# Moving a reload, a first norm and one weight's low parts in a two-block transformer kernel

## The reference

```python
def first_block(x, norm_gain, w_in, w_out, ...):
    xn = rms_norm(x, norm_gain)
    proj = einsum('bsd,de->bse', xn, w_in)
    qa, ka, va, za, qi, ki, wi, qb, kb, vb, zb = split(proj)
    a_out = dsa_attention(qa, ka, va, qi, ki, wi, bias_a)      # top-k chosen keys
    b_out = dilated_attention(qb, kb, vb, bias_b)
    mixed = concatenate([a_out * silu(za), b_out * silu(zb)])
    return x + einsum('bse,ed->bsd', mixed, w_out)

def second_block(x, ...):
    h = rms_norm_2(x, norm_mix)
    q_flat, kv_flat, g_attn, u_pool, g_merge = split(h @ w_in)
    a = nsa_attention(...) @ w_branch_attn
    b = pool_mixer(u_pool, pool_w, pool_scale) @ w_branch_pool
    ga, gb = split(sigmoid(g_merge))
    x = x + (ga * a + gb * b) @ w_out
    h = rms_norm_2(x, norm_mlp)
    x = x + square(relu(h @ w_ff1)) @ w_ff2
    return rms_norm_2(x, norm_final)
```

## Time and profile before

| | us |
|---|---|
| median of 3 executions | 1024.54 (1023.99 to 1026.65) |
| the profiled execution | 1024.92 |
| its span, first to last instruction | 1022.9 |
| TensorE busy | 1007.9 |
| VectorE busy | 679.3 |
| ScalarE busy | 555.7 |
| GpSimd busy | 419.5 |

### The profile page before, as it was taken

One profiled execution on the slowest core, in us unless ns is written; L12 is line 12 of the kernel. 1 busy time (PEld: TensorE's weight loads), 2 busy tenths in 40 slices (PEclk: granted clock), 3 DMA queues, 4 the chain that ended last, 5 costly groups with the idle time before them and its releaser, 6 DMA issues.

```text
span 1022.9 us, 14244 instructions
## 1 busy us (share of the span) xinstructions
PE 1007.9 (99%) x5158; PEld 828.9 (81%) x5158; DVE 679.3 (66%) x1201; ACT 555.7 (54%) x1013; POOL 419.5 (41%) x403
## 2 busy tenths in 40 slices
PE   9999999999999999999999999999999999999997
PEld 7788877778777898878887778888888888888886
DVE  5578898788975356733477879354323325999997
ACT  8455444777862356544667874224433436654555
POOL 0023012666720003900254520007779865875563
PEclk9999999999999999999999999999999999999999
DMA  9533321337140384132200461239999951444552
GB/s 338 104 98 94 103 62 42 84 84 195 54 175 1 122 272 140 42 96 69 63 1 1 143 212 58 83 119 319 343 354 338 350 191 62 150 136 147 206 185 82
DMA packets 100165, 146.24 MB, mean 143 GB/s; under 512 B 6480, under 2 KB 60496, under 8 KB 100096
## 3 DMA queue, kind: packets, MB, share of 16 engines
q1 hardware_dynamic: 86800, 130.75, 39.6%
q10 hardware_dynamic: 12768, 12.88, 4.0%
q0 software_dynamic: 528, 1.70, 1.0%
HBM read 123.69 MB, written 21.63 MB: 142 GB/s over the span
## 4 chain that ended last, share of the span: by engine, by line
PE 87%; DVE 6%; ACT 3%; issue 2%; DMA 1%; POOL 0%; SPq 0%; ACTq 0%; DVEq 0%; POOLq 0%
PE bank L966 57%; PE bank L1478 5%; PE bank L1479 5%; PE bank L1480 5%; PE bank L1358 2%; PE bank L1148 2%; PE bank L1367 2%; PE bank L1119 1%; DVE x L2242 1%; PE bank L1381 1%; DVE stats L2241 1%; DVE u_lo L2144 1%; PE bank L1132 1%; DMA wring<-in_w_in 1%; PE bank L1268 1%
## 5 line engine op out<-in xcount | busy, mean ns | idle before, releaser
L2658 DVE TENSOR_TENSOR w_lo<-wring,w_hi 128x1024 fp32r<-128x1024 f32 x32 | 50.4, 1574 | 108.5 <-ACT w_hi L1997 108.5
L2144 DVE TENSOR_TENSOR u_lo<-wring,u_hi 128x1024 fp32r<-128x1024 f32 (+2 forms) x69 | 83.3, 1215 | 53.8 <-ACT u_hi L1652 53.1
L966 PE MATMUL bank<-u_hi,h_hi 128*128 128x512 f32 (+1 forms) x288 | 110.9, 385 | 0.1
L966 PE MATMUL bank<-u_hi,h_lo 128*128 128x512 f32 (+1 forms) x288 | 109.3, 379 | 0.0
L966 PE MATMUL bank<-u_lo,h_hi 128*128 128x512 f32 (+1 forms) x288 | 109.0, 379 | 0.0
L1652 ACT ACTIVATE u_hi<-wring 128x1024 fp32r<-128x1024 f32 (+1 forms) x64 | 66.2, 1034 | 71.1 <-PE bank L966 56.1
L966 PE MATMUL bank<-h_hi,w_hi 128*128 128x512 f32 (+2 forms) x272 | 103.2, 380 | 0.0
L966 PE MATMUL bank<-h_hi,w_lo 128*128 128x512 f32 (+2 forms) x272 | 103.2, 379 | 0.0
L966 PE MATMUL bank<-h_lo,w_hi 128*128 128x512 f32 (+2 forms) x272 | 103.2, 379 | 0.0
L966 PE MATMUL bank<-h_hi,u_hi 128*128 128x512 f32 x224 | 93.5, 417 | 0.4 <-ACT arena L1594 0.2
L966 PE MATMUL bank<-h_hi,u_lo 128*128 128x512 f32 x224 | 87.8, 392 | 0.0
(11 more groups left out here) (400 smaller groups left out, 2599.0 us busy)
## 6 DMA issues: line engine op xcount, KB each, us to landing
wring<-in_w_in SPq DMA_DIRECT2D x60, 512.0 KB, 3.9
wring<-in_w_ff ACTq DMA_DIRECT2D x12, 1024.0 KB, 8.6
wring<-sums_kept SPq DMA_DIRECT2D x16, 768.0 KB, 4.2
wring<-in_w_ff SPq DMA_DIRECT2D x22, 512.0 KB, 6.4
wring<-in_w_ff SPq DMA_DIRECT2D x32, 256.0 KB, 3.4
sums_kept<-wring SPq DMA_DIRECT2D x22, 256.0 KB, 5.0
wring<-in_w_out SPq DMA_DIRECT2D x2, 2048.0 KB, 13.3
wring<-in_w_ff SPq DMA_DIRECT2D x4, 1024.0 KB, 6.9
```

What stands on the lines that cost most here:

```text
L966: last = mm(b, lhs, rhs, start=(start and n == 0), stop=(stop and n == 2))
L2144: done = v.tensor_tensor(u_lo[raw_place(u)][:, cols], raw_unit(u)[:, cols], u_hi[hi_place(u)][:, cols].bitcast(F32), ALU.subtract)
L2658: v.tensor_tensor(cut(w_lo[ring3(m)]), src, cut(w_hi[ring3(m)]).bitcast(F32), ALU.subtract).then_inc(w_lo_done, 1)
```

## The change

Three things move, and no arithmetic is changed.

1. LOW1: the two halves of the low parts of unit F0 + 7 (gate tile za 3) are made in VectorE's iterations 52 and 54; before, in 50 and 52.
2. The first block's end. ScalarE loads the square root's table before the last half of mixed_high, and squares the first tile of x after one kv2 unit; before, after three. VectorE waits for x and adds the first tile's sums before any kv2 low part; the low part of U2 follows before the first norm, those of U2 + 1 and U2 + 2 after it.
3. The reload of x for the second block. Before, SyncE issued x's four loads, and then branch units 3 to 7. Now it issues unit 3, x's tile 0, unit 4, tile 1, unit 5, tile 2, unit 6, tile 3, unit 7.

```diff
     LOW1 = {4: (F0 + 1, 0), 6: (F0 + 1, 1), 12: (F0 + 2, 0), 14: (F0 + 2, 1), 22: (F0 + 3, 0), 24: (F0 + 3, 1), 30: (F0 + 4, 0), 32: (F0 + 4, 1),
-            38: (F0 + 5, None), 44: (F0 + 6, None), 50: (F0 + 7, 0), 52: (F0 + 7, 1)}
+            38: (F0 + 5, None), 44: (F0 + 6, None), 52: (F0 + 7, 0), 54: (F0 + 7, 1)}
...
                 if name == "w2o1":
-                    sp.wait_ge(pv_done, VALUES + NS)
                     sp.wait_ge(x_out, 16 * NT)
-                    for i in range(NT):
-                        sp.dma_start(x[:, i, :], x_kept[i]).then_inc(x_back, 16)
                     for e in range(3, KC):
                         load_branch(e)
+                        if e < 3 + NT:
+                            sp.wait_ge(pv_done, VALUES + NS)
+                            sp.dma_start(x[:, e - 3, :], x_kept[e - 3]).then_inc(x_back, 16)
...
+            nc.scalar.preload_act_table(ACT.Sqrt)
             mixed_high(7, slice(S // 2, S))
-            for u in range(HI_UNITS - 1):
+            high(U2)
+            squares(NT, 0, 0)
+            for u in range(1, HI_UNITS - 1):
                 high(U2 + u)
-            for i in range(NT):
-                if i >= 1:
-                    input_high("h2", i - 1)
+            for i in range(1, NT):
+                input_high("h2", i - 1)
                 squares(NT, 0, i)
...
             mixed_low(7, slice(S // 2, S))
-            for u in range(2):
-                low(U2 + u)
             dve.wait_ge(x_in, 16 * NT)
             for i in range(NT):
                 add_x(0, i, [0])
                 if i >= 1:
                     take_halves("h2", i - 1, V_G2, h_lo)
                 add_x(0, i, [1])
+                if i == 0:
+                    low(U2)
                 norm(NT, i, xn2)
                 if i == 0:
+                    low(U2 + 1)
                     low(U2 + 2)
```

## The result

The changed kernel takes 1028.01 us (median of 7 executions, 1027.22 to 1030.78) against 1024.54 us (1023.99 to 1026.65, 7 executions): a ratio of 1.0035, with a 95% interval of 1.0023 to 1.0047. It is 3.5 us slower. That is just over the 0.3% (1027.6 us) that the forecast called the edge of "no change", and inside its range of 1023.6 to 1028.6. The likeliest value, 1026.1, is 1.9 us too low, and the measured one lies above that case's own range (1025.0 to 1027.0).

A forecast was written before the change was run, and what follows sets the result against it. The prediction took TensorE to bound the kernel, busy 1007.9 of 1022.9 us. Its terms, -0.5 + 3.6 - 0.9 - 0.6 = +1.6 us on the median of 1024.54, gave 1026.1 us; 8-in-10 range 1023.6 to 1028.6.

The forecast's parts named there:

- Part 1, what goes: Iteration 50: without the moved half, turned_low starts earlier and TensorE's 1.04 us wait shrinks; -0.5 us, bounds 0 and -1.04.
- Part 1, what comes: Iteration 54: TensorE's gate fill waits for the moved half, which VectorE makes behind scores, gate rows and mixed_low; +3.6 us.
- Part 2: First block's end: x's first tile is normalized earlier, so TensorE's wait on line 1015 goes; -0.9 us, bounds 0 and -0.9.
- Part 3: Reload of x: branch unit 3's second half lands sooner, so TensorE's wait on br_lo goes; -0.6 us, bounds -0.6 and 0.
- The sum without the clock: Whole kernel: all gains and the new stall, +1.6 us on the median, 1026.1 us, with nothing for half rate.
- The clock falls: Rival: behind iteration 54's gap TensorE's matmuls run at half rate, costing 3.75 us more, 1029.9 us; chance 0.12.
- The likeliest case: Whole kernel: the sum as made, 1026.1 us, by itself 1025.0 to 1027.0; chance 0.64.
- the wait on u_lo: Sign of being right: a TensorE wait of 3 to 4.4 us near 267, its longest, for VectorE's low parts.
- a clock of 0.5 behind the stall: Sign of being wrong: granted clock at 0.5 after iteration 54's new wait, where 1.0 around 271 was expected.
- the case of missing gains: Rival: the stall comes but the gains do not; +2.4 to +3.6 us, 1026.9 to 1028.1 us; chance 0.14.

The follow-up runs named there:

- Part 2 alone: The kernel before with only the first block's end changed: 1023.03 us, ratio 0.9981.
- part 3 alone: The kernel before with only the reload of x moved between the branch units: 1025.03 us, ratio 1.0001.
- LOW1 alone: The kernel before with only the gate weight's low-part halves moved to iterations 52 and 54: 1031.93 us, ratio 1.0067.
- the gap filled: The changed kernel with 14 extra, overwritten 128x512 matmuls in TensorE's iteration 54 before its wait for the gate unit's low parts: 1025.54 us, ratio 1.0003.
- x's tiles one unit later: The changed kernel with the gate unit's low parts made whole in iteration 52 and x's tiles loaded behind branch units 4 to 7: 1022.68 us, ratio 0.9973.
- the whole unit in iteration 52: The changed kernel with the gate weight's low parts made in one subtraction in iteration 52: 1022.61 us, ratio 0.9976.
- the half behind the scores: The changed kernel with the second low-part half in iteration 54 right behind VectorE's two score rows: 1026.01 us, ratio 1.0011.

## Why the forecast held in part, point by point

- **Part 1, what goes** (-0.5): -0.59 us measured, by the mechanism given.
- **Part 1, what comes** (+3.6): 3.41 us measured, at the instruction and for the reason given. The reading of the two queues was right.
- **Part 2** (-0.9): the wait went, with 3.5 us of room where 4 were forecast. Part 2 alone gains 1.75 us in the median, not 0.9. Two things lie in the difference. Its profile has no wait on br_lo, which is 0.6, 0.7 and 0 us in three profiles of the kernel before. And of the 80 executions of the kernel before that were timed beside the experiments, 28 took 1026.1 us or more, most of them in a cluster some 2.5 us above the others; with part 3 alone it is 4 of 12. Of the 56 ordinary executions of the five versions with the new block's end and no long stall, one did. So the long executions go with the old block's end. Their recorded mean clock is lower too: 0.995 to 0.996 for the four above 1029 us, 0.997 to 0.999 for the 24 from 1026.1 to 1027.6, 0.998 to 1.000 for the rest. Both fit what the run with LOW1 alone shows, a longer wait on line 1015 with a fall of the clock; no long execution of the kernel before was profiled, so it is not shown.
- **Part 3** (-0.6): 0 by itself, the bound given. The reason given with it (x shares the transfer) is not shown: unit 3's half took 4.8 us to land in that run and 3.1 to 4.1 us in the others with this order.
- **The sum without the clock** (1026.1 us): 1025.54 us measured, with the gap filled.
- **The step that failed** is the chance and the price of "The clock falls". The likeliest case counted nothing for the clock. By the forecast's own signs, the wait on u_lo came as foretold, and so did a sign of being wrong, "a clock of 0.5 behind the stall". The forecast gave it 0.12, because at the kernel's end TensorE "kept the clock through the first 2 us", and so took one place's rest for what a rest is allowed to last. The runs show no such length. At the end of the kernel before, the last matmul is over at 1016.9 (not 1018, as the forecast has it) and the clock falls at 1020.9 (a mean of 0.97 over the next us), 4.0 us later; in its second profile 4.5 us lie between (1016.3 and 1020.8). Over the ends of all 14 profiles this time goes from 2.1 us (1014.7 to 1016.8, x's tiles one unit later) to 5.3 us (1014.9 to 1020.2, the whole unit in iteration 52). In the gap of the changed kernel it is 3.1 us, and with the half behind the scores the clock fell although TensorE had resumed after 2.2. A gap of 3.6 us lay amid these. On the rows of before alone (4.0 us) that was open; with all of them the rival deserved more than even odds. It came true. Its price was too high per event, 3.75 us; it measures 1.6 us in the profile (3.1 us of work at half rate) and 2.5 us in the median. The median is above the profile, and three of the seven executions took 1029.3 to 1030.8 us. An estimate: had those the 6.8 us at half rate seen with the half behind the scores, they would take (6.8 - 3.1) / 2 = 1.9 us more than the profiled 1027.48, 1029.3. No profile of such an execution exists, and the mean clocks recorded for the seven (0.994 to 0.998) don't sort them by time.
- **Luck.** That the result lies inside the range is luck in part. The range's upper end, 1028.6, stood for the case of missing gains; with the clock at the forecast's own price, 1029.9, the time would lie outside. It is inside because the clock cost 1.6 to 2.5 us and not 3.75.

The sentence that was cited beside that rival (the Trainium skill, TensorE: Matmul & The Clock Gate, "HAM oscillation — how this bites in real kernels") names waits of a few microseconds as enough to bring half rate back. By that rule, the traces agree: the clock fell in the wait of 3.4 us. It also fell with waits of 2.4 and 2.2 us. With the price measured afterwards, that rival would have put the sum at 1026.1 + 1.6 = 1027.7, close to the 1028.0 measured; with the forecast's own price it gave 1029.9.

What stays open: why loads issued in the same order take 7.6 us to land in one execution and 8.7 us in another, and what the long executions of both kernels do.

## What to carry to other kernels

Before a preparing step is put an iteration later, find the first instruction that waits for it and the place of each in its own queue: here 0.2 us of slack stood against a delay of 3.6 us, and both could be read off the trace of before. Where TensorE is 99% busy, price each new rest of some 2 us or more twice, as the rest and as work at half rate behind it (here 1.6 to 3.4 us in the profiles). Don't take one rest that kept the clock for proof that the next one will: at the kernel's end it held for 2.1 to 5.3 us. Time the parts of a mixed change apart: here two of three edits gained 2 us together, and the third took 5.3 back.

## What was not expected of the hardware

- The clock can fall after TensorE is at work again: behind a gap of 2.2 us it fell 1.3 us into the work and stayed at 1.2 GHz for 6.8 us. Behind a gap of 3.4 us it fell in the gap, and was back 3.1 us into the work. Of the six falls amid work that were profiled, five kept 1.2 GHz for 3.4 us (before the matmuls resumed and behind that together) and this one for 6.8 us.
- In one execution it fell among small waits early in the kernel. In the profiled execution with the gap filled (1027.79 us, where the others of that kernel took 1025.1 to 1025.8) a load came late, and TensorE waited twice for 0.7 us among small matmuls. Its windows there:

```profile
24.00:25.00 1.00, 0.29 (x3) 0.14 (x1) 1.00 (x5) 1.00 (x4) 0.00 (x0) 0.86 0.97 352
25.00:26.00 1.00, 1.00 (x5) 1.00 (x6) 0.72 (x2) 1.00 (x3) 0.00 (x0) 0.50 0.24 87
26.00:27.00 1.00, 1.00 (x6) 1.00 (x5) 1.00 (x3) 0.98 (x3) 0.00 (x0) 0.50 0.03 13
```

In this one execution, a load late by a microsecond and a half thus goes with about 2.3 us more (1027.79 against the usual 1025.5).
- The same VectorE subtraction of 128x512, both inputs in SBUF, took 0.68 us alone and 1.50 us beside a GpSimd instruction that had 0.95 us left to run, whichever of the kernel's subtractions stood there.
